# Padding each slot of the rounded weights and of their rests by 96 bytes, in a float32 transformer stack on one Trainium2 core

## The reference

```
proj = rmsnorm(x) @ w_in                       # 2048 x 7168
x = x + mix @ w_out                            # 2048 x 2048
x = x + memory_attention(rmsnorm(x) @ w_mq, rmsnorm(mem) @ w_mkv) @ w_mo
x = x + (silu(a) * b) @ w_down                 # a, b: halves of conv(rmsnorm(x) @ w_up), 2048 x 11264
u = rms_norm(x) @ w_in_2
x = x + rms_norm(concat(y_a, y_b, y_c) @ w_out_2)
x = x + rms_norm((silu(gate) * val) @ w_down_2)
```

## Time and profile before

| | |
|---|---|
| Median of 3 runs | 2634.1 us (2633.75 to 2635.73) |
| The profiled execution, its own time | 2635.15 us |
| Its span, first to last instruction | 2633.4 us |
| Granted TensorE clock, mean | 0.999 of full speed |
| TensorE matmul busy | 2621.2 us |
| VectorE busy | 1789.2 us |
| ScalarE busy | 1345.3 us |

### The profile page before, as it was taken

One profiled execution on the slowest core, in us unless ns is written; L12 is line 12 of the kernel. 1 busy time (PEld: TensorE's weight loads), 2 busy tenths in 40 slices (PEclk: granted clock), 3 DMA queues, 4 the chain that ended last, 5 costly groups with the idle time before them and its releaser, 6 DMA issues.

```text
span 2633.4 us, 41690 instructions
## 1 busy us (share of the span) xinstructions
PE 2621.2 (100%) x15689; PEld 2316.8 (88%) x15689; DVE 1789.2 (68%) x2188; ACT 1345.3 (51%) x1647; POOL 150.8 (6%) x106
## 2 busy tenths in 40 slices
PE   9999999999999999999999999999999999999999
PEld 9888898889999888888888889998888888888887
DVE  7677567566645777777775456998777777776444
ACT  6554375464533655555553344444665555554443
POOL 2001200000200200000001222000020000000000
PEclk9999999999999999999999999999999999999999
DMA  8555455546535555555555555655565555556554
GB/s 264 193 160 186 140 184 186 176 156 203 184 130 169 188 193 188 189 190 188 188 191 191 189 189 180 200 198 166 173 193 190 189 188 189 191 191 207 192 191 146
DMA packets 256256, 487.12 MB, mean 185 GB/s; under 512 B 15069, under 2 KB 80629, under 8 KB 255616
## 3 DMA queue, kind: packets, MB, share of 16 engines
q1 hardware_dynamic: 254496, 476.11, 54.7%
q0 software_dynamic: 1488, 9.19, 1.0%
q10 hardware_dynamic: 144, 0.01, 0.0%
HBM read 483.12 MB, written 2.13 MB: 184 GB/s over the span
## 4 chain that ended last, share of the span: by engine, by line
PE 92%; DVE 5%; ACT 1%; POOL 1%; issue 1%; DMA 0%; SPq 0%; DVEq 0%; ACTq 0%; POOLq 0%
PE ps L2107 92%; DVE w_lo L1325 2%; DVE acc L1854 2%; POOL sumsq L724 1%; DMA raw<-in_weights 0%; ACT w_hi L784 0%; DVE ua L1359 0%; DVE ya L1918 0%; DVE x_res L2088 0%; ACT lnz L1219 0%; PE ps L2640 0%; PE ps L2427 0%; DVE y_lo L1390 0%; DVE ya L1920 0%; DVE pa L1883 0%
## 5 line engine op out<-in xcount | busy, mean ns | idle before, releaser
L1325 DVE TENSOR_TENSOR w_lo<-raw,w_hi 128x1024 fp32r<-128x1024 f32 x899 | 1117.6, 1246 | 767.4 <-ACT w_hi L784 766.1
L2107 PE MATMUL ps<-op,w_hi 128*128 128x512 f32 (+1 forms) x6208 | 1615.0, 350 | 0.7 <-DVE op L1398 0.6
L784 ACT ACTIVATE w_hi<-raw 128x1024 fp32r<-128x1024 f32 x899 | 949.0, 1059 | 1083.3 <-PE ps L2107 1051.0
L2107 PEld LDWEIGHTS ps<-op,w_lo 128*128 128x128 f32 x5024 | 944.5, 188 | 163.8
L2107 PE MATMUL ps<-op,w_lo 128*128 128x256 f32 x5024 | 1086.7, 278 | 0.0
L2107 PEld LDWEIGHTS ps<-op,w_hi 128*128 128x128 f32 x6208 | 939.0, 188 | 5.2 <-issue 2.8
L2107 PE MATMUL ps<-g,w_hi 128*128 128x512 f32 x704 | 219.6, 393 | 0.0
L2107 PE MATMUL ps<-w_hi,g 128*128 128x512 f32 x704 | 218.3, 391 | 0.0
L2107 PE MATMUL ps<-w_hi,op 128*128 128x512 f32 x512 | 164.5, 396 | 0.0
L2107 PEld LDWEIGHTS ps<-g,w_lo 128*128 128x128 f32 x704 | 132.4, 188 | 30.0
L2107 PEld LDWEIGHTS ps<-w_hi,g 128*128 128x128 f32 x704 | 132.3, 188 | 27.9
(11 more groups left out here) (318 smaller groups left out, 1535.0 us busy)
## 6 DMA issues: line engine op xcount, KB each, us to landing
raw<-in_weights SPq DMA_DIRECT2D x899, 512.0 KB, 4.3
x_res<-in_x SPq DMA_DIRECT2D x8, 256.0 KB, 6.1
mem_x<-in_mem POOLq DMA_DIRECT2D x1, 2048.0 KB, 8.4
x_res<-in_x POOLq DMA_DIRECT2D x1, 2048.0 KB, 9.7
w_row<-row_dram POOLq DMA_DIRECT2D x2, 1024.0 KB, 7.4
out_x<-x_res SPq DMA_DIRECT2D x3, 512.0 KB, 2.9
rel_rev<-rel_dram POOLq DMA_DIRECT2D x1, 1024.0 KB, 7.7
hg_con<-in_hg_consts POOLq DMA_DIRECT2D x1, 576.0 KB, 5.3
```

What stands on the lines that cost most here:

```text
L784: nc.scalar.activation(w_hi[:, s], raw[:, s], ACT.Copy).then_inc(hi_rounded, 1)
L1325: TT(w_lo[:, s], raw[:, s], w_hi[:, s].bitcast(F32), ALU.subtract).then_inc(chunk_split, 1)
L2107: return nc.tensor.matmul(out, lhsT, rhs, start=start, stop=stop, skip_group_check=True)
```

## The change

The two tiles get 24 more float32 columns, 96 bytes, in each slot, and are then used as a view that leaves these columns out. Slot s of each tile begins s x 4192 bytes after the tile's start, where it began s x 4096 bytes after it. No instruction is added, removed or reordered, and no shape changes. `raw` stays as it was. `w_lo` moves by 4 x 96 = 384 bytes and every tile after it by 768.

```
+SLOT_PAD = 24
...
-        w_hi = place("w_hi", [P, SLOTS, CW], F32R)
-        w_lo = place("w_lo", [P, SLOTS, CW], F32R)
+        w_hi = place("w_hi", [P, SLOTS, CW + SLOT_PAD], F32R)[:, :, 0:CW]
+        w_lo = place("w_lo", [P, SLOTS, CW + SLOT_PAD], F32R)[:, :, 0:CW]
```

## The result

The changed kernel takes 2659.84 us (median of 4 runs, 2659.64 to 2659.97), the kernel before 2634.36 us in the same comparison. The ratio is 1.0096, with a 95% interval of 1.0078 to 1.0113: 25.5 us slower, outside of the predicted range. I had given 0.87 to no change and 0.08 to slower.

What follows compares the result with a forecast made beforehand. The prediction took TensorE's pace as the bound. All terms were taken as 0: 2635.15 + 0 = 2635.2 us for an execution like the profiled one, 2634.1 against the median, 2634.3 forecast; range 2631.8 to 2639.0.

Steps and rivals of the forecast that it cites:

- What bounds the kernel: TensorE's pace sets the time; it holds 92% of the chain that ended last, VectorE 5%.
- TensorE's weight loads and matmuls on the slots: New slot starts change a load by -2 to +2 ns, judged from float32 loads; 0 taken.
- the missing row: No profile row has the rounded stream at a start like the new ones; named among the prediction's weakest places.
- The three pairs: TensorE against slot writers, slot against slot, weight load against the matmul beside it: searched for conflicts by place.
- The eight matmuls of squares: Column sums of squares, no slot taking part: 230 ns each, as slow as the 228.3 with slots.
- Writers against TensorE: In the first `up`, ScalarE and VectorE writing slots don't change TensorE's step; any conflict under 3 ns a matmul.
- The tiles behind: `x_res`, `op` and the arena move by 768 bytes, keeping their place within 64 bytes; 0 taken.
- the subtraction: VectorE's `w_lo` subtraction in the second layer's mixers: 0.9 us either way, 0 taken; rival beyond 0.2%, chance 0.02.
- the rounding: ScalarE's rounding spreads from 1042 to 1068 ns, ahead of chunks TensorE reaches later; 26 ns of it cost nothing.
- A dearer start, slower: Slots 1 to 3 off 128-byte multiples need one more access: at 1 ns a matmul 11.1 us, 2646 us; chance 0.07.
- A relief in TensorE's reads: Slot operands at equal places modulo 4096 collide; padding lifts it for slots 1 to 3, faster from 5.3 us; chance 0.04.
- The forecast's reason: Slots begin at different places, but place along a partition chooses nothing that matters: the same 2634.3 us.

Runs made afterwards that it cites:

- the 10 ns ahead of slot 1: Slot 1 of `w_hi` 96 bytes off, slots 2 and 3 512 bytes later, against the kernel before: 2647.73 us, ratio 1.0049.
- distances of 128: The changed kernel's layout, but each slot at a multiple of 128 bytes (slots 4224 apart), measured against the kernel before: 2650.88 us, ratio 1.0065.
- half of the change: Only `w_lo`, or only `w_hi`, at slot distances of 4192, all else kept modulo 512, against the kernel before: 2667.79 and 2667.75 us, both 1.0126.

## Why the prediction was wrong

**What bounds the kernel** was right. TensorE's pace sets the end, and the whole loss is a loss of that pace at an unchanged clock.

**The step that failed** is "TensorE's weight loads and matmuls on the slots", which I costed at nothing, "-2 to +2 ns, 0 taken". No run shows that 0. In its place the runs showed 25.5 us over the 11,136 matmuls on slots 1 to 3 (of the 14,848 that take the 900 x 6144 = 5,529,600 columns of the chunks), 2.3 ns each on the mean. The bound came from loads of float32 operands, whose matmuls run at about half the pace (two with `pa` of 256 columns take 0.43 us at 1722.21); and it looked at where one operand starts, when what counts is where it starts against the other. I had named the missing row as the weakest place, and then still gave 0.87 to nothing happening.

**The three pairs** were read rightly and too far. The first two comparisons are at one and the same distance: slots at 4096 from each other, weight columns at 512, activations at 2048 or 1024, so every pair of weights and activations is 192 bytes apart modulo 512. Equal pace over such pairs says that a multiple of 512 bytes is harmless, which the run with slots 4608 apart confirmed (0.9999), and nothing of other distances. The eight matmuls of squares lie at a distance of 0 modulo 512 (`ones_r` and the squares both begin at 320), and at 230 ns each showed that TensorE goes no faster where no slot takes part. No layout brought a form below 2.72 us a chunk. What a layout could win at most was not shown by any trace or run. From "no gain to be had here" I went to "no loss to be had either", and this does not follow. The kernel before stood at the best distance found for the together form, which has 568 of the 900 chunks, and for these there was only a way down. For the tokens form there was a better one (2.72 for 2.747), and for the whole form two layouts without the spells of 2.83. The earlier trace rows show 0.34 us a step of the whole form in one place; 40 us later the same trace has 0.35.

**Writers against TensorE**: right as far as seen. In the timeline after, slot 0 keeps 0.34 us while other slots are written and read.

**The tiles behind, the subtraction, the rounding** at nothing. For the tiles behind, the sum was right and the reason wasn't: moving them and `w_lo` alone gave 1.0007 (0.9997 to 1.0017), but as 6.3 us won in the whole form and 7.0 lost in the tokens form. The subtraction in the mixers is within a few ns:

```profile
L1326 DVE TENSOR_TENSOR w_lo<-raw,w_hi x48: 1214/1221/1229, 1691.7 to 1829.8; 128x1024 fp32r<-128x1024 f32 x48
```

The stage is a little longer, so the count differs from the 46 of the earlier trace rows; 1221 for 1215 ns is 0.3 us.

**The sums.** The upper end of the range is added wrong, 2636.6 + 2.8 being 2639.4 and not 2639.0; 2659.84 is outside of both. The prediction also let VectorE set the pace from 1677 to 1807 us. The chain that ended last does run through it there, but TensorE's whole-form chunks show no wait in that stretch, and what hung on VectorE was the wait of 1.7 us in `out_2`.

**The rivals.** "A dearer start, slower" had the right sign, the right engine and the right trace of itself in the profile (slots 1 to 3 slower, slot 0 as before), at 0.07 and with 1 ns for 2.3. Its mechanism was wrong: with all tiles 96 bytes off, 1.0001. "A relief in TensorE's reads" had what the runs bear out, reads of one engine whose pace goes by their distance, though not the equal places modulo 4096 (0.9999 with slots 4608 apart), and the wrong sign for this change. Had I joined the two, the price would have been open to both sides.

**The forecast's reason**, that the place along a partition chooses nothing that matters, was my assumption, and the runs speak against it: 64 bytes on `op` alone changed the whole form from 2.72 to 2.88 us. No run shows another engine's accesses slowing TensorE's, but by these runs the places of its two operands are not independent in their effect. At their best the matmuls take 113.3 ns for 256 columns and 226.7 for 512 (2.72 us over 24 and over 12 matmuls), so the time goes with the columns.

**What stays open.** The experiments show that the distance between TensorE's two operands acts: activations moved against the slots by 64 bytes, 1.0068, everything moved by 96, 1.0001. Slots spaced by 4224 cost the whole form nothing (though `w_lo` alone moved by 128 took 2.76 us), multiples of 512 bytes cost no form anything (0.9999), and a shift of `w_hi` by odd multiples of 128 costs the together form (2.809 us for 2.773). The order of the matmuls matters to it (2.827 for 2.773). That it is the weight load which meets the matmul running beside it is argued from this and from the 10 ns ahead of slot 1, not shown: no run took the load away. Distance is not all: the whole form takes 2.72 or 2.83 us a chunk at the same places, and slots that haven't moved can be slower behind or between moved ones (2.83 with `w_hi` alone padded, 2.791 with distances of 128). So TensorE's pace also depends on what went before. What picks it, and why half of the change costs more than all of it, is open. Untested, too, is the layout that these runs suggest, `w_lo` moved by 128 bytes against `w_hi` for the whole form with the tokens form's activations placed for themselves.

## What to carry to other kernels

Before moving a tile that TensorE reads, work out the distance modulo 512 bytes (multiples of 512 changed nothing here, 0.9999) between each matmul's stationary and moving operand, and keep it or test others; 32 to 96 bytes cost up to 7% of the pace here (2.90 for 2.72 us a chunk), and which is best differs with the form and with the order of its matmuls. Read the pace of a form in all of its stretches, not in one: the same instructions at the same places had two paces here, 4% apart. A view that shows equal pace over many operands is evidence only for the distances that occur among them. When a cause is ruled out as the source of a loss, it has not been ruled out as the source of a further one.

## What the runs showed of the hardware

- A shift of 64 bytes of the activations against the weights took the form with 256 columns from 2.72 (at its faster pace) to 2.88 us a chunk (5.9%) and the form with 512 moving weight columns from 2.747 to 2.72.
- The form with 256 columns took 2.72 us a chunk in 63 chunks of the kernel before and 2.83 in 46, at the same clock and with all tiles in the same places; it changed only at interruptions.
- A shift of all tiles together by 96 bytes (1.0001), and slots of `w_hi` 512 bytes further apart (0.9999), did nothing that could be measured.
- The least time in any form was 2.72 us for 6144 columns at a granted clock of 1.00, 113.3 ns for a matmul of 256 columns and 226.7 for one of 512, in whatever place.
- None of the fourteen other layouts and orders was measurably faster than the kernel before; the best, with only the tokens form's activations moved, stood at 0.9992 (0.9983 to 1.0001).
